# One core, hybrid decoder step: page strips side by side, a fifth page slot, and the input's second half turned between the first Q matmuls

## What is computed

```python
up = rmsnorm(hp, mix_norm[i]); us = rmsnorm(hs, mix_norm[i])
q, k, v = diff_qkv(up, w_qkv[a])                      # 8 heads, 2 sub-heads of 128, values 256 wide
o_real = lax.map(lambda qb: diff_attend(qb[0], qb[1], ((k, v, pos_p),), lam, slopes), (q_blocks, pos_blocks))
qs, kn, vn = diff_qkv(us, w_qkv[a])
k_past = cache_k[a, page_table].reshape(b_s, past_len, N_HEADS, 2, HEAD_DIM)   # 8 x 16 pages of 128 keys
v_past = cache_v[a, page_table].reshape(b_s, past_len, N_HEADS, V_DIM)
o_s = diff_attend(qs, pos_new, ((k_past, v_past, pos_past), (kn, vn, pos_new)), lam, slopes)
# diff_attend: (softmax1 - lam*softmax2) @ v, causal, with ALiBi
```

## Time and profile before

| | us |
|---|---|
| median of three runs | 3187.7 |
| profiled execution | 3186.87 |
| its span, first to last instruction | 3185.1 |
| PE busy (share of the span) | 3103.1 (97%) |
| DVE busy | 1507.0 (47%) |
| ACT busy | 1065.2 (33%) |
| POOL busy | 278.3 (9%) |
| DMA, mean over the span | 200 GB/s |

### The profile page before, as it was taken

One profiled execution on the slowest core, in us unless ns is written; L12 is line 12 of the kernel. 1 busy time (PEld: TensorE's weight loads), 2 busy tenths in 40 slices (PEclk: granted clock), 3 DMA queues, 4 the chain that ended last, 5 costly groups with the idle time before them and its releaser, 6 DMA issues.

```text
span 3185.1 us, 59411 instructions
## 1 busy us (share of the span) xinstructions
PE 3103.1 (97%) x25406; PEld 2913.4 (91%) x25406; DVE 1507.0 (47%) x2160; ACT 1065.2 (33%) x1502; POOL 278.3 (9%) x226
## 2 busy tenths in 40 slices
PE   8999999999988899999999999999999999999998
PEld 8987877787766699999999999999999999999998
DVE  4344444444444454444444444447544444445445
ACT  3233333333333433223222323225333233233333
POOL 0022222222210010000000000004000000000002
PEclk9999999999999999999999999999999999999999
DMA  6469999999998545444444444443444444444442
GB/s 199 147 237 366 362 353 359 373 359 359 361 331 310 193 140 167 137 147 141 146 142 137 144 147 134 146 146 102 145 144 148 152 149 150 148 155 148 146 152 94
DMA packets 341938, 637.98 MB, mean 200 GB/s; under 512 B 11528, under 2 KB 257775, under 8 KB 308367
## 3 DMA queue, kind: packets, MB, share of 16 engines
q1 hardware_dynamic: 337120, 620.67, 55.9%
q0 software_dynamic: 3328, 11.24, 1.0%
q10 hardware_dynamic: 1230, 2.29, 0.2%
HBM read 625.37 MB, written 9.23 MB: 199 GB/s over the span
## 4 chain that ended last, share of the span: by engine, by line
PE 88%; DVE 5%; ACT 3%; issue 2%; DMA 2%; SPq 0%; POOL 0%; ACTq 0%; DVEq 0%; POOLq 0%
PE ps L1688 71%; PE ps L1804 7%; PE ps L1852 3%; PE ps L1829 3%; DVE halves L1121 1%; ACT halves L815 1%; DMA raw<-in_cache_k_dram 1%; PE ps L1957 1%; DVE pa_n L1414 1%; PE ps L1937 1%; PE ps L2100 0%; DVE pa_s L1408 0%; ACT pa_s L953 0%; DMA io_tm<-in_x_sample_dram 0%; PE ps L1842 0%
## 5 line engine op out<-in xcount | busy, mean ns | idle before, releaser
L1121 DVE TENSOR_TENSOR halves<-raw,halves 128x2048 fp32r<-128x2048 f32 x300 | 687.9, 2293 | 667.3 <-ACT halves L815 667.2
L1688 PE MATMUL ps<-xhi,halves 128*128 128x320 f32 (+1 forms) x3840 | 861.7, 311 | 4.6 <-DVE halves L1121 2.4
L815 ACT ACTIVATE halves<-raw 128x2048 fp32r<-128x2048 f32 x300 | 573.4, 1911 | 867.9 <-PE ps L1688 860.8
L1688 PE MATMUL ps<-yhi,halves 128*128 128x336 f32 x2816 | 657.2, 318 | 0.1
L1688 PEld LDWEIGHTS ps<-xhi,halves 128*128 128x128 f32 x3840 | 649.9, 188 | 6.0 <-issue 4.8
L1688 PE MATMUL ps<-xlo,halves 128*128 128x320 f32 (+1 forms) x1920 | 598.2, 312 | 0.0
L1688 PEld LDWEIGHTS ps<-yhi,halves 128*128 128x128 f32 x2816 | 483.1, 188 | 0.5 <-issue 0.4
L1688 PE MATMUL ps<-ylo,halves 128*128 128x336 f32 x1408 | 447.2, 318 | 0.0
L1308 DVE TENSOR_SCALAR keyT<-ps 128x512 f32<-128x512 f32 x256 | 177.0, 692 | 463.4 <-PE ps L1804 463.4
L1688 PE MATMUL ps<-hA_hi,halves 128*128 128x336 f32 (+1 forms) x1408 | 375.6, 314 | 2.9 <-DVE hT L1579 2.8
L1688 PE MATMUL ps<-hB_hi,halves 128*128 128x336 f32 (+1 forms) x1408 | 372.8, 312 | 0.0
(11 more groups left out here) (224 smaller groups left out, 3076.0 us busy)
## 6 DMA issues: line engine op xcount, KB each, us to landing
raw<-in_w_gate_up_dram SPq DMA_DIRECT2D x176, 1024.0 KB, 5.1
raw<-in_cache_k_dram SPq DMA_DIRECT2D x124, 1024.0 KB, 6.8
raw<-in_cache_v_dram SPq DMA_DIRECT2D x121, 1024.0 KB, 8.3
raw<-in_w_down_dram SPq DMA_DIRECT2D x88, 1024.0 KB, 5.0
kv_raw<-in_w_qkv_dram SPq DMA_DIRECT2D x64, 512.0 KB, 8.4
raw<-in_w_qkv_dram SPq DMA_DIRECT2D x16, 1024.0 KB, 5.1
raw<-in_w_o_dram SPq DMA_DIRECT2D x16, 1024.0 KB, 5.4
page<-in_cache_v_dram SPq DMA_DIRECT2D x7, 1024.0 KB, 7.2
```

What stands on the lines that cost most here:

```text
L815: act.activation(whi[t][:, :], raw[r][:, :], ACT.Copy).then_inc(hi_ready[t], 1)
L1121: dve.tensor_tensor(wlo[t][:, :], raw[r][:, :], whi[t][:, :].bitcast(F32), ALU.subtract)\
L1688: mm = pe.matmul(out, l, r, start=first and n == 0, stop=last and n == 2)
```

## The change

The page loop runs over t = 0 ... 129. In a step PE now turns the first half of key page t, does one projection chunk (or `turn_block`), `tile_back`, `tile_turn`, the second half, `turn_probs`, `turn_new_probs`, `turn_out`, `join_halves`, `tile_scores`, `tile_values`, the other projection chunk, then `scores(t)`, `values(t - 6)`, `new_values` and `new_scores`. There is one `keyT`; its place in SBUF goes to a fifth page slot (seven from key page 116). The last four pages of probabilities are turned together in the last step, and their values follow. New tokens, pairs and `turn_back` start one or two steps earlier; the five row loads stand in steps 113, 114, 115, 116 and 118 of the POOL list. ACT and DVE lists are put in the new order. In the input stage chunks 8 to 15 are turned one by one from the second to the ninth chunk of the first Q block, and weight unit 0 is converted behind chunk 7.

```diff
-SLOTS = 6
+SLOTS = 7
-STEPS = PAGES + VALUE_LAG
+STEPS = PAGES + 2
+def turned_in(t):
+    first = [v for v in (t - TURN_LAG,) if 0 <= v < PAGES - GROUP]
+    return first + (list(range(PAGES - GROUP, PAGES)) if t == STEPS - 1 else [])
+def valued_in(t):
+    if t < PAGES:
+        return [v for v in (t - VALUE_LAG,) if v >= 0]
+    return [PAGES - VALUE_LAG, PAGES - VALUE_LAG + 1] if t == PAGES else list(range(PAGES - GROUP, PAGES))
-NEW_AT = {114 + n: n for n in range(NB)}
-PAIR_AT = {124 + 2 * p: p for p in range(3)}
-HX0 = 124
+NEW_AT = {113 + n: n for n in range(NB)}
+PAIR_AT = {122 + 2 * p: p for p in range(3)}
+HX0 = 122
+BACK_AT = (113, 114, 115, 116, 118)
...
-        keyT1 = place("keyT1", [P, UNIT], F32, z); z += UNIT * 4
+        page4 = place("page4", [P, UNIT], F32, z); z += UNIT * 4
+        pages = raw + [page4] + late
-        keyT = [place("keyT0", [P, UNIT], F32, z), keyT1]; z += UNIT * 4
+        keyT = place("keyT", [P, UNIT], F32, z); z += UNIT * 4
...
-                if t == KV_STEPS * (H - 1) + 1:
...
+                if t in BACK_AT:
+                    row_back(BACK_AT.index(t))
```

ACT and, in the same way, DVE, where weight unit 0 is converted:

```diff
-                if c == 3:
+                if c == 7:
                     split_hi(U_Q)
```

`keys_out` on ACT, and in the same way on DVE:

```diff
-                if t >= 2:
-                    act.wait_ge(s_full, t - 1)
-                act.activation(keyT[t % 2][:, 512 * g:512 * g + 512], ps[g % 2][:, :], ACT.Copy)\
+                if t:
+                    act.wait_ge(s_full, t)
+                act.activation(keyT[:, 512 * g:512 * g + 512], ps[g % 2][:, :], ACT.Copy)\
```

The new list of a step on ACT:

```diff
+            for t in range(STEPS):
+                if t < PAGES:
+                    keys_out(t, 0)
+                if t - 1 in NEW_AT:
+                    new_exps(NEW_AT[t - 1])
+                if t in KV_END:
+                    kv_rows(KV_END[t])
                 if tile_at(t, 4) is not None:
                     tile_squares(tile_at(t, 4))
+                if t < PAGES:
+                    keys_out(t, 2)
                 if tile_at(t, 3) is not None:
                     tile_turned(tile_at(t, 3))
                 if tile_at(t, 5) is not None:
                     tile_features(tile_at(t, 5))
+                for v in turned_in(t):
+                    if v < PAGES - GROUP:
+                        probs_out(v)
+                if t - 1 in NEW_AT:
+                    new_probs_out(NEW_AT[t - 1])
+                for n in range(9, 4 * KV_BLOCKS):
+                    if KV_FIRST[n - 1] == t:
+                        kv_split_hi(n)
```

On DVE:

```diff
+            for t in range(STEPS):
+                if t in KV_END:
+                    kv_features(KV_END[t])
+                if t < PAGES:
+                    keys_out(t, 1)
...
+                if t in KV_END:
+                    kv_rows(KV_END[t])
                 if tile_at(t, 5) is not None:
                     tile_normed(tile_at(t, 5))
...
+                if t < PAGES:
+                    keys_out(t, 3)
...
+                if t in PAIR_AT:
+                    factors(PAIR_AT[t])
...
+                if t < PAGES:
+                    scores_out(t)
+                if t < PAGES and t % GROUP == GROUP - 1:
+                    maxima(t // GROUP)
```

The input on PE:

```diff
-            for c in range(DC):
+            for c in range(8):
                 turn_in(c)
+            def first_ready(cc):
+                if 0 < cc < 9:
+                    turn_in(7 + cc)
+                pe.wait_ge(*chunk_done(0, cc))
+            fm_block(U_Q, 0, 0, (0, 1), first_ready, 0)
```

The new list of a step on PE:

```diff
+            for t in range(STEPS):
+                work = list(KV_AT.get(t, ()))
+                if t < PAGES:
+                    turn_keys(t, 0)
+                if t in KV_END:
+                    turn_block(KV_END[t])
+                elif work:
+                    project(*work.pop(0))
+                if tile_at(t, 5) is not None:
+                    tile_back(tile_at(t, 5))
                 if tile_at(t, 3) is not None:
                     tile_turn(tile_at(t, 3))
                 if HX0 <= t < HX0 + 8:
                     turn_back(2 * (t - HX0))
+                if t < PAGES:
+                    turn_keys(t, 1)
+                for v in turned_in(t):
+                    if v < PAGES - GROUP:
+                        turn_probs(v)
                 if t - 1 in NEW_AT:
                     turn_new_probs(NEW_AT[t - 1])
...
                     tile_scores(tile_at(t, 0))
                 if tile_at(t, 3) is not None:
                     tile_values(tile_at(t, 3))
+                if HX0 <= t < HX0 + 8:
+                    turn_back(2 * (t - HX0) + 1)
+                for block, cc in work:
+                    project(block, cc)
+                if t < PAGES:
+                    scores(t)
+                for v in turned_in(t):
+                    if v >= PAGES - GROUP:
+                        turn_probs(v)
+                for v in valued_in(t):
+                    values(v)
+                if t - 1 in NEW_AT:
+                    new_values(NEW_AT[t - 1])
+                if t in NEW_AT:
+                    new_scores(NEW_AT[t])
```

More of the change, by code:

```diff
@@ L100, in page_order @@
 def page_order():
-    order = [("k", n) for n in range(4)] + [("w", n) for n in range(3, 11)]
+    order = [("k", n) for n in range(4)] + [("w", n) for n in range(3, 11)] + [("k", 4)]
     for t in range(STEPS):
-        if 4 <= t + 1 < PAGES:
-            order.append(("k", t + 1))
-        if 0 <= t - VALUE_LAG:
-            order.append(("v", t - VALUE_LAG))
+        if 5 <= t < PAGES:
+            order.append(("k", t))
+        order.extend(("v", v) for v in valued_in(t))
         for n in range(11, 4 * KV_BLOCKS):
@@ L120, in page_slots @@
 def page_slots():
-    last, turns, out = {i: None for i in range(4)}, {i: 0 for i in range(SLOTS)}, []
+    last, turns, out = {i: None for i in range(5)}, {i: 0 for i in range(SLOTS)}, []
     for n in range(len(IN_STEPS)):
         if n == MORE_FROM:
-            last.update({4: None, 5: None})
+            last.update({5: None, 6: None})
         slot = min(last, key=lambda i: -1 if last[i] is None else last[i])
@@ L313, in trunk @@
         aT_new = place("aT_new", [P, 2, 144], F32, hT_at)
-        pages = raw + [place(f"page{i}", [P, UNIT], F32, x_at + 3 * D * 4 + i * UNIT * 4) for i in range(2)]
+        late = [place(f"page{5 + i}", [P, UNIT], F32, x_at + 3 * D * 4 + i * UNIT * 4) for i in range(2)]
         assert 3 * D * 4 + 2 * UNIT * 4 <= 2 * DC * T * 4
@@ L633, in _ @@
                     sp.wait_ge(split_ready[half_slot], half_turn + 1)
+                elif slot == RAW:
+                    sp.wait_ge(unit_used[1], 9)
                 else:
@@ L1443, in _ @@
             dve.wait_ge(cleared, 5)
-            for t in range(-1, STEPS):
-                if t + 1 < PAGES:
-                    keys_out(t + 1, 1)
+            for t in range(STEPS):
[4 more added lines that the diff above has]
+                if t in NEW_AT:
+                    if NEW_AT[t]:
+                        dve.wait_ge(n_full, NEW_AT[t])
+                    queries(NEW_SEQ[NEW_AT[t]], 2, qn_set)
+                if t in KV_END:
+                    kv_rows(KV_END[t])
                 if tile_at(t, 5) is not None:
                     tile_normed(tile_at(t, 5))
-                if t in KV_END:
-                    kv_features(KV_END[t])
                 if t - 1 in PAIR_AT:
                     out_means(PAIR_AT[t - 1])
-                if t + 1 < PAGES:
-                    keys_out(t + 1, 3)
-                if 0 <= t < PAGES:
-                    scores_out(t)
-                if t in KV_END:
-                    kv_rows(KV_END[t])
-                if 0 <= t < PAGES and t % GROUP == GROUP - 1:
-                    maxima(t // GROUP)
+                if t < PAGES:
+                    keys_out(t, 3)
+                if t - 1 in NEW_AT:
+                    new_sums(NEW_AT[t - 1])
                 if tile_at(t, 4) is not None:
@@ L1821, in scores @@
                     pe.wait_ge(s_out, t)
-                if t - TURN_LAG > 0:
-                    pe.wait_ge(pt_out, t - TURN_LAG)
-                turned = sum(at + 1 < t for at in NEW_AT)
-                if turned:
-                    pe.wait_ge(nt_out, turned)
+                if 0 <= t - TURN_LAG < PAGES - GROUP:
+                    pe.wait_ge(pt_out, t - TURN_LAG + 1)
                 for b, a, j in score_strips():
```

114 lines of the change are left out of this document (36 added, 78 removed).

## The result

The changed kernel takes 3201.98 us as a median of 13 executions (3191.28 to 3206.9), the kernel before, measured with it, 3188.66 (3186.58 to 3192.95, also 13). The ratio is 1.0034, with a 95% interval of 1.0026 to 1.0041: slower by a third of a per cent. The profiled execution took 3196.67 us, 9.8 more than the profiled one of before; it is one of the shorter of its thirteen. The first group lies 4 us above the kernel before, not 13; what the other has is taken up at the end.

What follows compares the result with a forecast made beforehand. TensorE sets the pace, DMA close behind. Input +2.9, page-stage opening -0.5, six periods +11.4 and tail -10.8 make +3.0 on the profiled 3186.87: 3189.9 us, stated as 3190.5 for the median; range 3170 to 3208.

Steps and rivals of the forecast that it cites:

- The switches: Plain page step: scores and values together save tiling-mode edges, 6.05 to 5.75 us; -4.8 us per sixteen steps; winning rival: 0.22.
- The waits in a period: Sixteen page steps: TensorE reaching inputs early adds 8.3 us, old waits give back 1.6; with -4.8 saved, +1.9.
- tile values: Prompt tiles' value matmuls at steps r = 4, 9, 14: now wait for `pa_t`, 0.59, 0.75 and 0.58 us.
- the second half turn of r = 3 and 13: Second half of the key turn there: waits grow to 1.0 and 0.8 us, behind POOL's later subtraction.
- r = 11: Step 11 of sixteen: tile scores wait 0.68 us for the previous tile's features, `tile_back` 0.41 for its input.
- r = 6: Step 6 of sixteen: tile scores wait 0.68 us for the previous tile's features, `tile_back` 0.41 for its input.
- The single key tile: Scores need same-step key copies: covered by 0.1 us until step 112; rival of uncovered copies: +18 us, 3208, chance 0.14.
- The input: Stage before the pages: later squares and `split_lo` delay the second Q block to 44.5, +2.9 us (-1 to +4).
- The tail: Last page steps up to the output projection: less page stall and half clock, -10.8 us (-16 to -2).
- the joins behind `factors`: End of the tail: four loop rounds less, but joins wait for `factors`; net -0.5 us.
- The uncovered key copies: From step 112 no projection covers them: about 0.85 us waited before scores, 0.5 before the second half turn.
- the spells at half clock: Tail: some 3.4 us lost to half clock would go, with 12.1 idle: -15.5 us together.

## Why the prediction was right where it was, and wrong where not

The time, 3202, lies in the range (3170 to 3208) and 11.5 above the value. The direction was left open by it, with 0.35 for slower by over 0.2%; that is what happened. By its steps:

- **The switches** held: a plain step of 5.75 forecast, 5.74 measured, 6.01 with two edges put back. TensorEngine Tiling (Array Packing), section Tiling Modes, of the Trainium skill has the rule that a change of tiling mode drains the engine, and these runs agree. That the sum is right to the hundredth is luck in part: the first half turn and the turn of probabilities took 0.08 less each than forecast, the two halves of the projection 0.08 more each. That scores behind a projection cost no more than behind keys was my assumption and came out so: the last projection matmul is followed after 0.24 where its neighbours stand 0.155 apart, 0.09 for the edge.
- **The waits in a period** were forecast as +1.9 with the switches taken off, and are +1.4. The list of waits makes it look like less: a period of after has 5.6 us of listed waits where before had 1.2, 4.4 more. Switches and listed waits alone would give -0.4. Twelve waits stand there instead of five, and seven more at the 0.24 found above, beyond the listed length, are 1.7 of the missing 1.8. I had costed each place by distances of starts and so had this in without knowing it. One credit was too large: I took off 1.6 for the waits of before, and 1.2 are listed there. By places: tile values 0.59, 0.75, 0.58 forecast, 0.59, 0.75, 0.57 gained by moving them; the second half turn of r = 3 and 13 forecast to wait 1.0 and 0.8, measured 0.99 and 0.76 (2.84 and 2.61 against 1.85); r = 11 0.68 + 0.41 forecast, 1.16 gained; r = 6 the same 1.09 forecast, 0.79 gained.
- **The single key tile** did not decide, as forecast: six waits, 3.6 us, all from step 112 on.
- **The input**: the second Q block was forecast for 44.5 and began at 44.72. The term was too small all the same, 2.9 for 4.5: the block began 3.1 later than before; having waited 1.67 us there, TensorE went on at half clock, matmuls 0.28 apart until about 48, where before they stand 0.155 apart from the start, and that costs the other 1.4.

```profile
44.72 0.50 PE L1720 MATMUL ps<-xhi,halves 128*128 128x336 f32 x1 [1.67 <-DVE gains L1183]
45.01 0.48 PE L1720 MATMUL ps<-xlo,halves 128*128 128x336 f32 x1
```

- **The tail** is the step that failed: -10.8 forecast, -2.2 measured. Some 4 us of that belong to this execution: two runs with practically the same code in the tail, the old input and the negation's form, have 142.5 and 143.2 instead of 147.1, so -6 to -7 against 149.3. The kernel before, its waits of TensorE in the tail:

```profile
PE ps L1906 <- DVE stage L1384: 7.2, 4, 2.1
PE ps L1881 <- ACT run L915: 7.1, 8, 0.9
PE ps L1804 <- DMA page<-in_cache_k_dram: 4.9, 1, 4.9
PE ps L1913 <- DVE o_n L1394: 4.7, 2, 3.6
```

With 4.1 us for other key pages and 2.1 for value pages, pages had 11.1 there and have 3.4 after: the stall shrank about as I said, and the 7.1 for the new exponentials went. What I set at -0.5, the joins behind `factors`, was the mis-sized term: the waits of `join_halves` and `turn_out` grew from 11.9 to 17.4 us, +5.5. `tile_back` waits 5.0 in the tail where it waited 1.2; 1.8 of them are in step 118, behind new-token work on VectorE, which I had not looked at. The uncovered key copies, which I had charged, are 5.6. I also let the spells at half clock go with the stall, and they did not: the granted clock of the whole tail is 0.93 before and 0.94 in the window above. The run with the pairs rearranged has 11 to 15 us less there, and part of it may have been there to gain in the kernel before, whose pairs waited 11.9; no run tried that.

With the tail as forecast the profiled execution would have been within 2 us of the 3189.9 forecast for it; that closeness is luck in part, since the page steps came out 4.3 us below their terms and the input and the end 2.5 above. The median is another matter: 3202 is 5 us above the profiled one. The two kernels with all edits that differ only in the queue of the rows show where such differences can arise, far behind anything that the change touches. Windows of the first, in the pooling stage between the feed-forward blocks:

```profile
2130.00:2140.00 10.00, 7.88 (x45) 7.65 (x46) 3.40 (x7) 2.61 (x5) 2.29 (x2) 0.71 0.00 0
2140.00:2150.00 10.00, 10.00 (x46) 10.00 (x46) 2.54 (x5) 2.45 (x6) 0.00 (x0) 0.50 0.01 2
2150.00:2160.00 10.00, 10.00 (x54) 10.00 (x53) 3.04 (x6) 2.96 (x7) 0.00 (x0) 0.59 0.00 0
```

and of the second, the same work:

```profile
2128.00:2138.00 10.00, 7.91 (x69) 7.68 (x69) 4.54 (x10) 3.80 (x8) 2.29 (x2) 1.00 0.01 2
2138.00:2148.00 10.00, 9.05 (x78) 8.91 (x76) 5.50 (x11) 5.12 (x12) 0.00 (x0) 1.00 0.00 0
```

In both TensorE was idle for 2.1 us in the first of these windows. In the one it ran for some 24 us at 0.5 (1.2 GHz; 0.71 and 0.59 are mixtures of the two levels), in the other at 1.0 (2.4 GHz), and all behind the start of w_o took 2125.0 against 2113.3 us. Of the traces here three show the spell in full (2125 us behind the start of w_o), two a shorter one (2118 and 2120), all in this stage. That the eight longer executions of after had it is likely, from their size and from their mean clock of 0.990 to 0.993 against 0.995, but none of them was traced. The kernel before is not free of it: on record with these runs it has 3204.73 once at a clock of 0.990 and 3199.74 once at 0.991, among well over sixty executions. Why it is rare there and frequent in the kernel after stays open.

## What to carry to other kernels

When small dependent steps are moved in front of their inputs to bring like work together, cost each by the distance from the moment its input exists to its new place, and add to a listed wait the stretch by which the next matmul would have started ahead of the last one's end; then try them behind the next long piece of work before giving up the order: here that turned a loss of 0.3% into a gain of 0.9%. Look for short operations whose duration jumps with what another engine does; one 2-column operation was worth 10 us. Before two medians a few us apart are compared, look at the granted clock of the single executions. A pipeline's end has its own order of queues: read who stands ahead of the last reductions on each engine.

## What was not expected of the hardware

- A VectorE operation on two columns is held to the end of POOL's 2.4 us operation (to 2.17 us for 0.17), as tensor_scalar from SBUF and as scalar_tensor_tensor with both inputs there; with its source in PSUM it takes 0.15 at the same moment.
- The same stage, with the same wait of 2.1 us ahead of it, ran at full clock in one execution and for some 24 us at half clock in another, 12 us apart.
- A wait of TensorE for a small input costs some 0.24 us more than its listed length (1.7 us for seven of them in a period; 0.17 and 0.25 for two read by distances of starts), because matmuls overlap and the list counts from the end of the last one.
